# Strassen in every second row pair of the FFN up product, with results and gated product in PSUM

## The reference

```python
def causal_dwconv(x, w, b):            # three taps, back 2, 1, 0
    k_w = w.shape[0]; s = x.shape[1]
    xp = jnp.pad(x, ((0, 0), (k_w - 1, 0), (0, 0)))
    return b + sum(w[k] * xp[:, k:k + s] for k in range(k_w))

def conv_ffn(x, w_up, w_conv, b_conv, w_down):     # x: 512 x 1024, w_up: 1024 x 5632
    h = causal_dwconv(x @ w_up, w_conv, b_conv)
    gate, val = jnp.split(h, 2, axis=-1)           # 2816 each
    return (jax.nn.silu(gate) * val) @ w_down
```

## Time and profile before

| | |
|---|---|
| time, median of 2 runs | 2191.52 us (2188.39 to 2194.66) |
| the profiled execution: its own time, span | 2195.75 us, 2194.0 us |
| mean granted clock of PE | 0.937 of 2.4 GHz |
| busy: PE, DVE, ACT, POOL | 89%, 67%, 46%, 39% |
| the four stretches of paired rows | 548.3 us of the span |
| DMA | 168.93 MB, mean 77 GB/s |

### The profile page before, as it was taken

How to read it: one execution, slowest core, us unless ns; L and a number is a source line. 1 busy time by engine, 2 the same in 40 slices (tenths; PEclk the granted TensorE clock), 3 DMA queues, 4 the chain that set the end, 5 groups by cost and what they waited for, 6 DMA issues and landing times.

```text
span 2194.0 us, 32813 instructions
## 1 busy us (share of the span) xinstructions
PE 1949.8 (89%) x12943; PEld 1674.9 (76%) x12943; DVE 1475.1 (67%) x1819; ACT 999.6 (46%) x1407; POOL 852.3 (39%) x366
## 2 busy tenths in 40 slices
PE   5999999989999998999967897789999967897887
PEld 4888888868778886874757787788887757887776
DVE  6125777762666667799589829985356589649984
ACT  4345777762555544442444424443223444324442
POOL 1222223242111112331356556654444355455652
PEclk8999999999999999999978898889999988997889
DMA  7210212131111111321211222222322212222221
GB/s 285 68 65 30 97 49 96 51 145 49 55 59 56 46 55 62 99 70 39 77 48 68 87 87 68 78 77 87 106 87 90 83 42 74 77 87 77 68 77 58
DMA packets 48841, 168.93 MB, mean 77 GB/s; under 512 B 5552, under 2 KB 7856, under 8 KB 48688
## 3 DMA queue, kind: packets, MB, share of 16 engines
q1 hardware_dynamic: 46384, 162.03, 21.9%
q10 hardware_dynamic: 2304, 4.81, 0.7%
HBM read 164.72 MB, written 2.10 MB: 76 GB/s over the span
## 4 chain that ended last, share of the span: by engine, by line
PE 37%; DVE 24%; issue 7%; ACT 4%; POOL 0%; DMA 0%; DVEq 0%; ACTq 0%
PE ps L619 12%; PE ps L620 11%; PE ps L621 11%; DVE cv L2538 7%; DVE Flo L1832 2%; DVE raw L2498 1%; DVE sq L2485 1%; DVE wS L2360 1%; DVE hf L1832 1%; ACT cv L1221 1%; DVE cv L1838 1%; DVE X L1838 1%; DVE wS L1832 1%; ACT sq L1221 1%; PE ps L936 1%
## 5 line engine op out<-in xcount | busy, mean ns | idle before, releaser
L1816 POOL TENSOR_TENSOR wlo<-raw,whi 128x1024 fp32r<-128x1024 f32 x241 | 613.0, 2554 | 902.0 <-ACT whi L1171 822.5
L619 PE MATMUL ps<-Zhi,whi 128*128 128x256 f32 x864 | 278.2, 322 | 127.6 <-DVE acc L2509 109.9
L1171 ACT ACTIVATE whi<-raw 128x1024 fp32r<-128x1024 f32 x167 | 174.1, 1058 | 323.2 <-PE ps L621 312.8
L619 PEld LDWEIGHTS ps<-Zhi,whi 128*128 128x128 f32 x864 | 195.1, 226 | 137.0 <-DVE acc L2509 117.1
L620 PE MATMUL ps<-Zlo,whi 128*128 128x256 f32 x864 | 271.8, 315 | 0.0
L621 PE MATMUL ps<-Zhi,wlo 128*128 128x256 f32 x864 | 270.5, 313 | 0.0
L2538 DVE SCALAR_TENSOR_TENSOR cv<-C,vec,cv 128x511 f32<-128x511 f32 (+1 forms) x144 | 246.9, 1775 | 14.1 <-ACT cv L1221 12.7
L620 PEld LDWEIGHTS ps<-Zlo,whi 128*128 128x128 f32 x864 | 195.2, 226 | 0.1
L621 PEld LDWEIGHTS ps<-Zhi,wlo 128*128 128x128 f32 x864 | 194.8, 225 | 0.0
L619 PE MATMUL ps<-Fhi,whi 128*128 128x512 f32 (+1 forms) x363 | 141.2, 389 | 0.0
L620 PE MATMUL ps<-Flo,whi 128*128 128x512 f32 (+1 forms) x363 | 140.4, 387 | 0.0
(11 more groups left out here) (351 smaller groups left out, 5388.0 us busy)
## 6 DMA issues: line engine op xcount, KB each, us to landing
raw<-in_units SPq DMA_DIRECT2D x299, 512.0 KB, 3.4
X<-in_xT SPq DMA_DIRECT2D x4, 512.0 KB, 9.4
X<-in_xT ACTq DMA_DIRECT2D x4, 512.0 KB, 5.2
out_xT<-X SPq DMA_DIRECT2D x8, 256.0 KB, 2.2
CX<-in_ctxT SPq DMA_DIRECT2D x4, 256.0 KB, 10.0
acc<-in_rope ACTq DMA_DIRECT2D x1, 384.0 KB, 3.1
...
```

The source lines that it names most:

```text
L619: nc.tensor.matmul(out, sh, mh, start=first, stop=False, skip_group_check=onto)
L1171: nc.scalar.activation(whi[:, plan.ring[s], :], raw[:, c % RAW, :], ACT.Copy).then_inc(sem("whi"), 1)
L1816: nc.gpsimd.tensor_tensor(wlo[:, plan.ring[s], :], src, whi[:, plan.ring[s], :].bitcast(fp32), ALU.subtract).then_inc(sem("wlo"), 1)
```

## The change

Of the Strassen rows every second one becomes classic again: rows 4, 6, 8 and 10 of the first half stay, and 1, 3, 5, 7 and 9 of the second, 18 in all; the 18 others are classic rows. Those are not computed from `B` but from the token forms (`from_forms`): an eighth quadrant X12 is kept, in high and low part, and a 512-column moving operand is two quadrants, that is two strips of 256 columns. A classic row signals its first 8 tiles by `gate`, by which the slot of its first unit is freed. A Strassen row's sums are written into its own PSUM tiles, in place of `C2`; the taps read PSUM; `silu`, the product and the low part work in PSUM as well (`halves`, `gated`, `low` with `src`), for classic rows too, so a tile is free when the low part is made. The order on ACT and DVE is written by row: a classic row together with the result sums of the Strassen row behind it, then that row's taps. The weight sums of the second half's first Strassen row stand after the down products, not among them, and so do the conversions. POOL makes each low part of a weight unit, and of a token form, in two instructions of 512 columns instead of one of 1024.

```diff
-X11, X21, X22, T1, T3, T2, T4 = range(7)
-SEVENS = [(l, f, j) for l in range(2) for f in range(2) for j in range(FH) if f or j >= PLAIN]
+X11, X21, X22, T1, T3, T2, T4, X12 = range(8)
+SEVENS = [(l, f, j) for l in range(2) for f in range(2) for j in range(FH) if j % 2 == f and (f or j >= PLAIN)]
...
-            tile(("ub", u), [("c12", u + 1)])
-            tile(("ua", u), [("c12", u + 1), ("c11", u + 1)], weights)
+            row = (2 * l + f) * FH + j
+            tile(("ub", u), [("c12", u + 1), low_of(row)])
+            tile(("ua", u), [("c12", u + 1), ("c2", u + 1), ("hf", hf_of(row))], weights)
...
-                    tile(("up", l, f, j), [("conv", 4 * ((2 * l + f) * FH + j + 1))],
+                    tile(("up", l, f, j), [low_of((2 * l + f) * FH + j)],
                          ktiles(f"up{l}", f * FH + j) + ktiles(f"up{l}", 2 * FH + f * FH + j))
+                    self.rows += 1
+                    if self.first[-1] % UT == 0:
+                        self.gate_unit[self.first[-1] // UT] = self.rows
...
-        Zhi, Zlo = place(14336, "Zhi", [7, HK, HT], fp22), place(21504, "Zlo", [7, HK, HT], fp22)
-        C2 = place(28672, "C2", [2, 2, T])
+        Zhi, Zlo = place(14336, "Zhi", [8, HK, HT], fp22), place(22528, "Zlo", [8, HK, HT], fp22)
+        ty = place(33280, "ty", [2, 2, T])
...
+            def from_forms(out, key, offset):
+
+                for k in range(KD):
+                    pair = slice(X11, X12 + 1, X12 - X11) if k < HK else slice(X21, X22 + 1)
+                    last = product(out.rearrange("p (i t) -> p i t", i=2), tuple(weights(key, offset + k)),
+                                   (Zhi[:, pair, k % HK, :], Zlo[:, pair, k % HK, :]), k == 0, k == KD - 1)
+                return last
...
-                        tile(("up", l, f, j))
+                        ps = tile(("up", l, f, j))
                         for part in range(2):
-                            last = linear(("up", l, f, j), Bhi, Blo, 0, SAT[f"ffn{l}"] + 1, XO, offset=KD * part,
-                                          ks=list(range(KD)), col0=T * part)
+                            if f == 0 and j < PLAIN:
+                                last = linear(("up", l, f, j), Bhi, Blo, 0, SAT[f"ffn{l}"] + 1, XO, offset=KD * part,
+                                              ks=list(range(KD)), col0=T * part)
+                            else:
+                                last = from_forms(ps[:, part * T:(part + 1) * T], ("up", l, f, j), KD * part)
+                            if part == 0:
+                                last.then_inc(sem("gate"), 1)
...
+                if was in plan.gate_unit:
+                    ac.wait_ge(sem("gate"), plan.gate_unit[was])
+                    return
...
-                act(Zhi[:, X11, k, :], y[:, 0, 0:HT], ACT.Copy, sem_name="zh")
+                act(Zhi[:, X11:X12 + 1:X12 - X11, k, :], y[:, 0, :].rearrange("p (i t) -> p i t", i=2), ACT.Copy, sem_name="zh")
...
-                act(C2[:, u % 2, 0, 0:HT], PS[plan.slot[n]][:, 0:HT], ACT.Copy, sem_name="c11")
...
+            def row_part(l, f, r, src, part):
+
+                j, c = (2 * l + f) * FH + r, (part * 2 + f) * FH + r
+                act(cv[:, j % 3, part, :], src, ACT.Identity, v_(f"ffn_b{l}", c), v_(f"ffn_w{l}", 88 + c), "ca")
+
+            def silu(l, f, r, gate, taps):
+
+                j = (2 * l + f) * FH + r
+                ac.wait_ge(sem("conv"), 4 * j + taps)
+                act(gate, cv[:, j % 3, 0, :], ACT.Silu, sem_name="se")
...
+            def classic_row(l, f, r, u):
+
+                n, j = plan.index["up", l, f, r], (2 * l + f) * FH + r
+                if u is None:
+                    psum(("up", l, f, r))
+                else:
+                    up_to(plan.pair_of["C", u])
+                    ac.wait_ge(sem("psum"), n + 1)
+                if f == r == 0:
+                    root(f"ffn{l}")
+                if u is not None:
+                    up_to(plan.pair_of["B", u])
+                if j >= 3:
+                    ac.wait_ge(sem("hf"), hf_of(j - 3))
+                if f == 0 and r < PLAIN:
+                    ac.wait_ge(sem("scaled"), PLAIN * l + r + 1)
+                gate, val = halves(l, f, r)
+                row_part(l, f, r, gate, 0)
+                row_part(l, f, r, val, 1)
+                if u is not None:
+                    first_part(u)
+                    up_to(plan.pair_of["B", u] + 1)
+                silu(l, f, r, gate, 2)
+                high(Fhi[:, r, :], val)
...
+            def seven_row(u):
 
                 l, f, r = SEVENS[u]
-                j = (2 * l + f) * FH + r
-                ac.wait_ge(sem("conv"), 4 * j + 4)
-                act(tmp[:, j % 2, 0:T], cv[:, j % 3, 0, :], ACT.Silu, sem_name="se")
+                gate, val = halves(l, f, r, u)
+                up_to(plan.pair_of["B", u] + 2)
+                ac.wait_ge(sem("c2"), u + 1)
+                row_part(l, f, r, val, 1)
+                ac.wait_ge(sem("c12"), u + 1)
+                row_part(l, f, r, gate, 0)
+                up_to(plan.pair_of["B", u] + 3)
+                silu(l, f, r, gate, 4)
+                high(Fhi[:, r, :], val)
...
+                        if (l, f, r + 2) in SEVENS:
+                            up_to(plan.pair_of["C", SEVENS.index((l, f, r + 2))])
...
-                            for s in range(first, first + 4):
-                                if m > 4 and s == converted[0] and plan.last[("split", plan.freed_by[s])] <= plan.index[("dn", l, f, m)]:
-                                    convert_next()
...
-                        nc.gpsimd.tensor_tensor(wlo[:, plan.ring[s], :], src, whi[:, plan.ring[s], :].bitcast(fp32),
-                                                ALU.subtract).then_inc(sem("wlo"), 1)
+                        for c in (slice(0, UT * P // 2), slice(UT * P // 2, UT * P)):
+                            lo = nc.gpsimd.tensor_tensor(wlo[:, plan.ring[s], c], src[:, c], whi[:, plan.ring[s], c].bitcast(fp32),
+                                                         ALU.subtract)
+                        lo.then_inc(sem("wlo"), 1)
...
+                if src is not None:
+                    tt(lo, src, hi.bitcast(fp32), SUB, "lo")
...
-                two = y[:, 1, :].rearrange("p (i t) -> p i t", i=2)
-                tt(Zlo[:, X11, k, :], y[:, 0, 0:HT], Zhi[:, X11, k, :].bitcast(fp32), SUB)
-                tt(Zlo[:, X21:X22 + 1, k, :], two, Zhi[:, X21:X22 + 1, k, :].bitcast(fp32), SUB, "zlo")
+                for i, pair in enumerate((slice(X11, X12 + 1, X12 - X11), slice(X21, X22 + 1))):
+                    mark(TTi(Zlo[:, pair, k, :], y[:, i, :].rearrange("p (i t) -> p i t", i=2),
+                             Zhi[:, pair, k, :].bitcast(fp32), SUB), "zlo")
+                need(("zlo", 2 * (HK * l + k) + 2))
...
-                mark(TTi(C2[:, u % 2, 1, :].rearrange("p (i t) -> p i t", i=2), both,
+                mark(TTi(y[:, T:2 * T].rearrange("p (i t) -> p i t", i=2), both,
...
-                mark(TTi(C2[:, u % 2, 0, HT:T], y[:, HT:T], wacc, SUB), "c12")
+                x, y = regions(u)
+                need(("psum", plan.index["ua", u] + 1), ("fW", u + 1))
+                mark(TTi(x[:, HT:T], y[:, HT:T], wacc, SUB), "c12")
...
+                    mark(STTi(y, halves[part][:, 0:T - back], v_(f"ffn_w{l}", 44 * (2 - back) + c), y, MUL, ADD), "conv")
...
+                tt(val, gate, cv[:, j % 3, 1, :], MUL, "hf")
+                queued(Fhi[:, r, :], Flo[:, r, :], src=val)
...
-                    if f == 0 and m == 3:
-                        u = SEVENS.index((l, 1, 0))
-                        sum_13(u)
-                        sum_2(u)
-                        sum_4(u)
...
+            def classic_row(l, f, r, u):
+
+                ps = psum(("up", l, f, r))
+                j = (2 * l + f) * FH + r
+                gate, val = ps[:, 0:T], ps[:, T:2 * T]
+                if f == r == 0:
                     ve.wait_ge(sem("n_rs"), 2 * NI[f"ffn{l}"] + 2)
-                scaled(ps, "scaled")
-                if r_ + 1 == PLAIN:
-                    used()
-                for part in range(2):
+                if f == 0 and r < PLAIN:
+                    scaled(ps, "scaled")
+                for part, src in enumerate((gate, val)):
                     ve.wait_ge(sem("ca"), 2 * j + part + 1)
-                    c = part * 2 * FH + r_
+                    c = (part * 2 + f) * FH + r
                     for back in (1, 2):
                         y = cv[:, j % 3, part, back:T]
-                        stt(y, ps[:, part * T:part * T + T - back], v_(f"ffn_w{l}", 44 * (2 - back) + c), y,
-                            MUL, ADD, "conv")
-                ve.wait_ge(sem("se"), j + 1)
-                b = to_split(T)
-                tt(b, tmp[:, j % 2, 0:T], cv[:, j % 3, 1, :], MUL, "hf")
-                queued(Fhi[:, r_, :], Flo[:, r_, :])
```

(62 more changed lines are left out.)

132 lines of the change are left out of this document (52 added, 80 removed).

## The result

The changed kernel takes **2015.84 us** (median of 2 runs, 2014.98 to 2016.7) against 2191.52: ratio 0.9198, 95% interval 0.9139 to 0.9257. That is 175.7 us less; the forecast was 150 less, 2041, with a range from 2019. The direction and the mechanism came as forecast. The profiled execution took 2016.7 us, its span is 2015.0 against 2194.0, 179.0 less.

A forecast was written before the change was run, and what follows sets the result against it. VectorE (DVE), held by POOL, was taken to bound the paired rows. Terms -173.9 + 5 + 13.5 + 0 + 2.6 + 3 = -149.8 from 2195.75, less the profiled run's offset, gave 2041 us, range 2019 to 2090.

The forecast's parts named there:

- (6): Low parts in two POOL pieces: +2.6 us, 0.22 at each of 12 PE waits; return counted as nothing, bound -5.
- (7): Token forms, first rows: the added quadrant lengthens DVE low parts and ACT copies; 5 us at most, 3 taken.
- (1): Four paired stretches: if PE never waits, the rows take 374.4 us against 548.3, 173.9 less.
- (3): Order inside a pair: smallest slack 1.3 us, at `first_sum`; small waits of 0.3 us a pair, 5 in all.
- (4): First Strassen row of each layer: does not gain from its 16.55 us; adds 13.5, 0 if freed.
- (2): Inside a pair: no other engine fills PE's 20.8 us; DVE 14.6, POOL 13.0 to 15.5, ACT under 15.
- (5): Classic rows' two-strip moving operand (`from_forms`): same columns stream, 0 taken; 3 us as upper case.
- (8): Sums moved behind the down products: a classic row of 11 us covers them; uncovered they would be 7 us.
- A: Rival: PE waits at `first_sum` in each pair, then half clock; 3.2 us a pair, 58 in all, 2094; chance 0.21.
- B: Rival: short holes at the Strassen rows lower PE's clock without a real wait; 24 us, 2065; chance 0.07.
- C: Rival: classic matmuls read the two-strip operand at half rate; +198 us, 2239, slower; chance 0.03.
- D: Rival: PSUM taps held like SBUF ones (7.0 us for 3.1), tail overruns its slack; 54 us, 2095; chance 0.03.

The follow-up runs named there:

- `one_piece`: The changed kernel with each of POOL's low parts (weights and token forms) as one instruction of 1024 columns again; 2028.52 us, ratio 0.9252.
- experiment 2: The kernel before with only POOL's low parts in two pieces, nothing else of the change; 2157.1 us, ratio 0.9848.
- `late1`: The changed kernel with one added DVE reduction (some 1.2 us) ahead of the first sum of every pair; 2018.71 us, ratio 0.9205.
- `late3`: The changed kernel with three added DVE reductions (3.73 us in the trace) ahead of the first sum of every pair; 2071.1 us, ratio 0.9443.
- `taps_sbuf`: The changed kernel with the Strassen rows' sums written to SBUF (`C2`) again and their taps read from there; 2013.16 us, ratio 0.9187.

## Why the prediction was right, and where it was wrong

The spans differ by 179.0, the forecast's sum is 149.8. By stages, from the starts of PE's first product in each:

| stretch | forecast | measured | difference |
|---|---|---|---|
| start to first FFN product, step (6) | +2.6 | 1068.8 to 1063.2: -5.6 | -8.2 |
| rows 0 to 3, both layers, step (7) | +3 | 67.65 to 68.1, 67.6 to 68.4: +1.25 | -1.75 |
| four paired stretches, steps (1), (3), (4) | -155.4 | 548.3 to 375.9: -172.4 | -17.0 |
| the rest (down products, mixer, end) | 0 | -2.2 | -2.2 |
| sum | -149.8 | -179.0 | -29.2 |

(The medians differ by 175.7: the profiled execution of the kernel before was 4.2 us above its median. Against the forecast time, 2041, the miss is 25 us.)

- **(6) failed, and it is the largest step behind the miss.** It charged the pieces +2.6 us, 0.22 at each of 12 waits for `wlo`, and let their return go as nothing, "bound -5 for five such places". The runs showed -12.7 us by the times (`one_piece`) and -10.6 by the profiled spans, so the term was mis-sized by 13 to 15 us, and its sign was wrong. The return isn't won "at one place". It is won along every stretch that is bound by DVE and has operations with two SBUF operands: the stage ahead of the FFN (165.8 us with one piece, 161.9 with two), the chain ahead of the first Strassen row (11.3 and 8.0), and, in the kernel before, the paired rows themselves (548.3 and 518.9, experiment 2).
- **(4) was mis-sized, mostly by the same cause.** It said that the first Strassen row of each layer, 16.55 us and held by the token forms, does not gain, and added 13.5. The reading of what holds it was right: with one piece PE waits there for `Zlo`, 5.1 us in two waits, and 4.5 in two in the kernel before. But it takes 12.71 us, for the pieces end that wait. With one piece rows 4 to 10 of both layers are 10.3 us above PE's price of 72.2 each; with two (74.43 + 73.10) they are 3.1 above, and what is left of it is half clock at the opening (0.76 in that row). So 13.5 was near the mark for single low parts, and the pieces took 7.2 of it away, less the 2.1 by which they lengthen rows 0 to 3. The prediction costed each part with the others absent.
- **(1), (2) right.** PE is the bound at its own price: 374.4 forecast, 375.9 measured, a pair 20.8 and 20.59. That the two sums are so near is in part luck: the second halves take 1.6 us less than PE's price and the first halves 3.1 more. DVE fills 13.86 us of a pair (14.6 forecast), POOL 14.42 (13.0 to 15.5), ACT 11.51 (under 15).
- **(3) right in its order, pessimistic in its 5 us.** At the second Strassen row of layer 0 `first_sum` ends at 1160.66 and PE comes to the product that needs it at about 1162.1, a slack of 1.4 (1.3 forecast). The low part of the first Strassen row ends at 1152.4 and the second one opens at 1155.03, a slack of 2.6 (2.3). A delay of 1.2 us at the smaller one costs nothing (`late1`). Within the slack there are no small waits at all: the second halves take 114.4 and 114.0, PE's price being 115.0. In the runs the wait for `first_sum` was in none of the pairs (`late1`) or in 17 of the 18 (`late3`).
- **The rule on the shared ports**, cited in (3) (the Trainium skill, SBUF — State Buffer, Who interferes with whom), holds for the single sums, `sum_13` 2.13 for 1.21, but its 5 us on top don't come: the tail stays within its slack, and in `taps_sbuf` a longer hold in the taps goes with a shorter one in the sum behind them. By the same rule the lock lasts for the whole of the instruction that came first, so shorter POOL instructions make each hold shorter; the worst tap fell from 2971 to 1795 ns (experiment 2). The prediction gave the rule's cost a figure, beside the sum, and its return none.
- **(5) right**: 0.2282 us per 512 columns from two strips. **(7) not seen**: with the added quadrant and single low parts rows 0 to 3 take 67.10 and 67.30 us (`one_piece`), against 67.65 and 67.6 before. The 1.25 us of the table come with the pieces, not with the quadrant. **(8) right**: the down products take 60.55 us, 60.59 before, and no row behind them waits.
- **Rivals.** A: its condition failed, and its price was close by chance (experiments 5 and 6). B: after the first Strassen row the clock stays at 1.00 in the stretches above, with its one dip at the opening (0.76). The Trainium skill (TensorE: Matmul & The Clock Gate, A second HAM failure mode: psum-queue depth-cycling) warns of brief idles between groups while PSUM tiles are cycled; the paired stretches have no such idles (113.99 us busy of 113.99), so they cannot show the effect, and the changed kernel does not suffer it. C is refuted by (5). D: the PSUM taps were never held, 748 to 753 and 736 to 750 ns. Even taps in SBUF take 4.82 to 4.89 us in the new pattern and not D's 7.0, and the time is the same.

The parts of the change by worth: pieces 10 to 13 us once the rest is there; every second row classic, with the new order and with PSUM as the source of the classic rows' taps and of all low parts, about 166, not taken apart; PSUM results for the Strassen rows 0 within 5 (the kernels without them are 2.7 and 3.3 us faster, within the intervals); and the Strassen rows that it keeps cost 26.6.

What stays open: how the preparation in rows 0 to 3 could be shorter (16.0 + 8.0 us a layer), which would have to cost less than 11.2 us a layer for nine Strassen rows to pay; how the 166 us divide among the row pattern, the order, and the PSUM sources of the classic rows' taps and of the low parts; and whether four pieces gain over the whole kernel.
